# The memory's layer norm in a PSUM bank, in three vector operations instead of two

## The chip, the cores and the metric

The kernel runs on one NeuronCore of a Trainium2 chip. The metric is the device time of one execution, in microseconds (us), lower is better. The engines are PE (TensorE: matmuls and transposes), DVE (VectorE), ACT (ScalarE), POOL (GpSimd) and SP (SyncE, which only issues DMAs). Each engine works through its own instructions in order and waits on semaphores. SBUF is the on-chip memory of 128 partitions; PSUM is a smaller one, in banks of 512 floats for each partition, into which PE writes.

## The reference

Two blocks follow each other: four layers with attention, attention to a fixed memory and a SwiGLU, then two layers of three gated attentions. All is float32, over 256 tokens of width 1024. What the change touches is the very first step on the memory (256 rows of width 1024), whose result all four layers of the first block use for keys and values:

```python
def layer_norm(x, g, b):
    xf = x.astype(jnp.float32)
    mu = jnp.mean(xf, -1, keepdims=True)
    var = jnp.mean(jnp.square(xf - mu), -1, keepdims=True)
    return ((xf - mu) * lax.rsqrt(var + LN_EPS) * g + b).astype(x.dtype)
...
m = layer_norm(mem, mem_ln_g, mem_ln_b)
# in each layer: m @ w_mem_kv[l] gives the keys and values of 4 heads
```

## The kernel before

Rows (tokens or memory rows) lie in two tiles of 128 partitions, `t` 0 and 1. Weights stream from HBM in *units* of two blocks of 128 rows by up to 512 columns. For a unit, SP loads `raw`; ACT rounds it into `w_hi` (task `split`, L1211); POOL takes the difference into `w_lo` (task `low`, two instructions of L1183 for a unit, each with both inputs in SBUF); PE multiplies it (task `products`, for each tile: L1417, L1418 and L1424, six matmuls). Unit n's load waits for the products of unit n-10, its split for those of unit n-8. An activation enters PE through a `turn_in` (four transposes, L1364, into one of two banks `tps`), ACT's `batch_hi` (L1219) and DVE's `take` (L1694).

Units 0 to 3 are the index queries (512 wide), 4 to 7 the index keys (328 wide), 8 to 11 a block of values (512), 12 to 15 the memory's keys and values for the first layer (512), 16 to 23 heads 256 wide.

The order of the work is not written by hand. `Plan.arrange` is a list scheduler: it knows a cost for each task and which tasks it follows, and takes again and again the task that can begin first (then by `prio`, then by its number) and puts it at the end of its engine's queue. A task that has a `room` must also find a bank that is free in the plan. The chip then runs these queues in order. Planned times steer only the order.

The memory's norm, `norm_tiles("mem_norm", ...)`, has for each tile a task `mem_norm_scale` (statistics and a Newton square root in tiny operations, L1813, L1585 to L1587, L1530 to L1534), then for each half of 512 columns a task `mem_norm` of two `scalar_tensor_tensor` (L1594, L1595), in place in the buffer of the memory's rows, which is the trace's `QT`. Each half is followed by a `turn_in`. In the plan before (planned times), DVE has: `mem_norm_scale` of tile 0, the first index queries' take, the index keys' evict and scale of tile 0, then `mem_norm` halves 0 and 1 at 29.91 to 31.51 and to 33.11, the index keys' evict and scale of tile 1, the take of the memory's first turn. PE has after unit 7's products of tile 1 (to 31.83): `turn_in` of the memory's half 0, unit 10 tile 0, unit 8 tile 1, unit 11 tile 0, unit 9 tile 1, `turn_in` of half 1, units 12 and 13 tile 0, unit 10 tile 1, unit 14 tile 0, unit 11 tile 1, `turn_in` of tile 1's half 0, unit 15 tile 0, `turn_in` of its half 1, units 12 and 13 tile 1, unit 16. Further on come eight index groups (L1376), whose scores DVE sums and searches in eight rounds for the top 64 (L1779 to L1802).

Of the kernel before, what the change touches and what calls it, by code (L numbers as in the profile page):

```python
# [11 lines left out]
ALU = mybir.AluOpType  # L12
# [4 lines left out]
T = 2  # L17
# [534 lines left out]
def plan(w):  # L552
# [8 lines left out]
    def norm_tiles(fn, gain, fed, source, chunks=None, keep=False, also=((), ()), scale=2300, apply=1600, acts="x"):  # L561


        done, taken = [], []
        for t in range(T):
            banks = [ch.units[0].mm[t] for ch in chunks] if chunks else None
            st = dict(t=t, gain=gain, banks=banks, keep=keep)
            first = p.task("DVE", "stage", Stage(fn + "_scale", fed[t], **st), scale, None, [*fed[t], *taken], prio=t - 1 if fn == "rms_pre" else 0)
            halves = []
            for half in range(2):  # L570
                one = p.stage(apply, fn, [gain.load, first, *also[t]], prio=t - 1 if fn == "rms_pre" else 0, half=half, **st)
                halves.append(one)
                if chunks and not keep:
                    banks[half].release = one
                if source is not None:
                    clear = [p.used["x"][t]] if acts == "x" else []
                    taken.append(p.tile_batches(source, 4 * half, 4, acts, 4 * half, t, [one], clear)[0].take)
            done.append(halves)
        gain.rest = [halves[1] for halves in done]
        if acts == "x":  # L580
            p.normed = len(p.units)
        return done
# [8 lines left out]
    for t in range(T):  # L591
# [7 lines left out]
    mem = p.task("SP", "mem", None, 3000, "mem_landed", prio=0, lat=2500, inc=16)  # L599
    g = p.gain("mem_ln_g", "mem_ln_b", None)  # L600
    g.load.prio = 0
    constants = p.task("SP", "constants", None, 500 * CONSTANTS, "prologue_landed", [g.load], prio=0, lat=8000,
                       inc=16 * CONSTANTS)
    norm_tiles("mem_norm", g, [[mem]] * T, "mem", scale=2500, acts="m")
    terms = p.task("DVE", "table_terms", None, 1200, "lambda_terms", [constants])
    powers = p.task("ACT", "table_exp", None, 1600, "lambda_exp", [terms])
    lambdas = p.task("DVE", "table_lambda", None, 700, "lambda_done", [powers])
# [8 lines left out]
    for l in range(DEPTH):  # L616
# [21 lines left out]
        if kind == 0:  # L638
# [3 lines left out]
            for t in range(T):  # L642
                bank = last.units[0].mm[t]
                st = dict(t=t, src=src, layer=j, banks=[bank])
                scale = p.task("DVE", "stage", Stage("index_keys_scale", [last.take[t]], **st), 2300, None,
                               [last.take[t]], prio=0)
# [58 lines left out]
        if kind == 1:  # L705
            steps = []
            for b in range(4):
# [4 lines left out]
                                  v=[(src, 2 * MIX + P * whole, P, 0, 0, 0),  # L712
                                     (src, 2 * MIX + P * part + at, HD, 0, 1, at)],
# [41 lines left out]
        g = p.gain("ln1_g", "ln1_b", l, vq[-1].units[-1].load)  # L755
        spec = [(c, n, "residual", c) for c, n in column_chunks(0, D)]
        if kind == 1:
            out = lin(w["w_out"][l], 8, "mixed", spec[:1], banks=[[(3,)], [(0,), (1,), (2,)]], hold=[[p.units[-1].mm[1]], [scored]],
                      rows=MIXED)
        else:  # L760
            out = lin(w["w_out"][l], 8, "mixed", spec[:1], banks=[[(0,)], [(1,)]], rows=MIXED)
        out += lin(w["w_out"][l], 8, "mixed", spec[1:], hold=[[scored]] * T, banks=ANY, rows=MIXED, closing=True)
        norm_tiles("layer_norm", g, [[ch.take[t] for ch in out] for t in range(T)], "x", out)


# [13 lines left out]
        g = p.gain("ln2_g", "ln2_b", l, up.units[-1].load)  # L779
# [5 lines left out]
        if l < DEPTH - 1:  # L785
            norm_tiles("layer_norm", g, fed, "x", down)
        else:
            ready = norm_tiles("layer_norm", g, fed, None, down, keep=True, apply=2300)
            x_in_banks = down
# [4 lines left out]
    for l in range(DEPTH_2):  # L794
        win = w["w_in_2"][l]
        g = p.gain("norm_pre_2", None, l, apart=[memory_last] if l == 0 else ())
# [18 lines left out]
        def branch(weight, mixed, gates, first, fed):  # L815
# [5 lines left out]
            for ci, (c, n) in enumerate(column_chunks(0, D)):  # L821
# [14 lines left out]
                      v=[(da, 1024 + P * i)], out=P * i, dv=P, flavour="differential", mask="bias",  # L836
# [11 lines left out]
        scale = p.task("DVE", "stage", Stage("latent_scale", bq.take, src=low, layer=l), 3400, None, bq.take)  # L848
# [5 lines left out]
        for t in range(T):  # L854
# [14 lines left out]
                      v=[(vm, HD * (2 * i + m), HD, m, 0, HD * m) for m in range(2)], out=[(0, i, 0, P)], scale=MLA_SCALE,  # L869
                      mask="causal", block=2, layer=l, mask_at=bias, z=(low, 416), z_fed=takes(bz))  # L870
                 for i in range(4)]
        for s in steps:
# [16 lines left out]
                      v=[(sw, 640 + HD * (i // 2), HD, m, 0, HD * m) for m in range(2)], out=[(0, i, 0, P)],  # L889
# [16 lines left out]
        g = p.gain("norm_post_2", None, l)  # L906
# [30 lines left out]
def build(nc, a, out):  # L937

    p = plan(a)
    order = p.order  # L940
    rel_rows = nc.dram_tensor("rel_rows", [BIAS_HEADS, P, REL_ROW], F32, kind="Internal").ap()

    with ExitStack() as ctx:
# [78 lines left out]
        ops = ctx.enter_context(nc.psum_tensor("ops", [P, 2, 512], F32))  # L1022
# [13 lines left out]
        def rows(src):  # L1036

            if src == "x":
                return x[:]
            if src == "tmp":  # L1040
                return tmp[:].rearrange("p (t c) -> p t c", t=T)
            if src == "H":
                return H[:]
            if src == "Y":
                return Y[:]
            if src == "mem":
                return QT[:].rearrange("p (t k) n -> p t (k n)", t=T)
            if src == "KI":
                return KI[:].rearrange("p (t c) -> p t c", t=T)
            if src == "MKV":  # L1050
                return MKV[:].rearrange("p (t c) -> p t c", t=T)
            name, cols, off = src
            buf = {"U": U, "tmp": tmp}[name]
            return buf[:, off:off + T * cols].rearrange("p (t c) -> p t c", t=T)
# [463 lines left out]
        def _(dve):  # L1518
            v = nc.vector
            chain = [0]  # L1520

            def link(ins):

                chain[0] += 1
                ins.then_inc(S["dve_chain"], 1)
                dve.wait_ge(S["dve_chain"], chain[0])
# [39 lines left out]
            HALF = (slice(0, D // 2), slice(D // 2, D))  # L1566
# [5 lines left out]
            def halves(g, half):  # L1572
                return [one if one is None else one[:, HALF[half]] for one in gains(g)]

            def norm_columns(t, keys):


                if keys:
                    return small[:, 7, 2 * t:2 * t + 2], small[:, 2, 2 + t:3 + t]
                return mean_var[:, 2 * t:2 * t + 2], rs[:, t:t + 1]  # L1580
# [9 lines left out]
            def norm_apply(t, src, dst, g, done=None, back=None, keys=False):  # L1590

                gg, bb = g
                mv, r = norm_columns(t, keys)
                link(v.scalar_tensor_tensor(out=src, in0=src, scalar=mv[:, 0:1], in1=gg, op0=ALU.subtract, op1=ALU.mult))  # L1594
                ins = v.scalar_tensor_tensor(out=dst, in0=src, scalar=r, in1=bb, op0=ALU.mult, op1=ALU.add)  # L1595
                if back is not None:
                    link(ins)
                    ins = v.bn_stats(back, dst)
                if done is not None:
                    ins.then_inc(done, 1)  # L1600
                else:
                    link(ins)
# [10 lines left out]
            def in_bank(st):  # L1613

                return acc[:, st.banks[-1 if len(st.banks) == 1 else st.half].slot[0], :]
# [69 lines left out]
            def gains(g):  # L1685
                dve.wait_ge(gain_landed[g.slot], g.need)
                return (Y[:, 0, :], None) if g.slot else (gain[:, 0, :], gain[:, 1, :])
# [116 lines left out]
            def do_stage(st, n):  # L1804
                done = S["stage"]
# [3 lines left out]
                fn, t = st.fn, st.t  # L1809
                if fn == "mem_norm_scale":  # L1810
                    m = rows("mem")
# [2 lines left out]
                    link(ins)  # L1814
                    norm_scale(t, stats[:, t, :, :])
                elif fn == "mem_norm":
                    m = rows("mem")[:, t, HALF[st.half]]
                    norm_apply(t, m, m, halves(st.gain, st.half), done)
                elif fn == "layer_norm_scale":
                    norm_scale(t, stats[:, t, :, :])  # L1820
                elif fn == "layer_norm":
# [22 lines left out]
                elif fn == "rms_post":  # L1844
                    z, c = in_bank(st), HALF[st.half]
# [18 lines left out]
                elif fn == "gain_z":  # L1864
                    z = rows(st.src)[:, t, 1536:2048].rearrange("p (h e) -> p h e", e=P)
# [4 lines left out]
                elif fn == "latent_scale":  # L1870
                    mv = small[:, 4, 0:4 * T]
# [217 lines left out]
```

## Time and profile before

| what | us |
|---|---|
| median of 3 runs | 1919.36 |
| lowest and highest | 1918.63, 1919.83 |
| the profiled execution | 1918.94 |
| its span, first to last instruction | 1917.1 |
| PE busy | 1867.1 (97%) |
| POOL busy | 1517.8 (79%) |
| ACT busy | 945.5 (49%) |
| DVE busy | 805.3 (42%) |

The span is what the engines' instructions cover, and the profiled execution has 1.8 us around it. A line such as `L1594 DVE SCALAR_TENSOR_TENSOR QT<-QT,small,gain` names the line of the kernel, the engine, the operation, and the buffer written and those read. `QT`, `L`, `U`, `small`, `gain`, `raw`, `x_rows` lie in SBUF; `acc`, `tps`, `ops` in PSUM.

### The profile page before, as it was taken

Reading aid. Unit: us, or ns where it says so; the run is one execution under the profiler, and the core shown is the slowest. Engines: PE = TensorE matmul, PEld = TensorE weight load, DVE = VectorE, ACT = ScalarE, POOL = GpSimd, SP = SyncE. Lnnn points to the kernel's source line nnn. Section 1 sums busy time; section 2 is a strip of 40 time slices with the busy share of each in tenths; the row PEclk is TensorE's granted clock in tenths of the full one; section 3 lists DMA queues with packets and bytes.
Section 4 is the critical chain, followed back from the end, with each engine's and each line's share of the span. In section 5 each row is a group of like instructions: output and inputs, shape, how many; then the busy total and the mean of one; then the engine's idle time right before and its main releaser. Section 6 shows DMA issues by size and latency. Waiting matters only on the chain.

```text
span 1917.1 us, 27395 instructions
## 1 busy us (share of the span) xinstructions
PE 1867.1 (97%) x9610; PEld 1529.6 (80%) x9610; DVE 805.3 (42%) x1929; ACT 945.5 (49%) x1501; POOL 1517.8 (79%) x1330
## 2 busy tenths in 40 slices
PE   7999999999999999999999999999999999999999
PEld 6778888877888887788888678887787887788877
DVE  6784110446311155411146741106757445455534
ACT  3554444354444355444435644434656654555743
POOL 6768989884897977698987779797686887777785
PEclk9999999999999999999999999999999999999999
DMA  8454656563766554465655456655564564555453
GB/s 274 132 153 149 194 154 232 180 194 102 208 196 214 176 187 139 145 189 147 238 161 149 153 163 186 196 195 166 173 181 130 157 205 153 164 170 176 132 175 110
DMA packets 184557, 330.54 MB, mean 172 GB/s; under 512 B 12220, under 2 KB 44520, under 8 KB 184424
## 3 DMA queue, kind: packets, MB, share of 16 engines
q1 hardware_dynamic: 176512, 323.21, 54.4%
q10 hardware_dynamic: 7912, 5.59, 1.0%
q8 instruction: 80, 1.31, 0.3%
q14 instruction: 53, 0.43, 0.1%
HBM read 325.35 MB, written 3.41 MB: 171 GB/s over the span
## 4 chain that ended last, share of the span: by engine, by line
PE 84%; POOL 5%; DVE 5%; DMA 2%; ACT 2%; issue 2%; SPq 0%; DVEq 0%; ACTq 0%
PE acc L1417 24%; PE acc L1418 23%; PE acc L1424 21%; POOL w_lo L1183 5%; PE tps L1364 4%; PE acc L1439 2%; PE acc L1420 2%; PE ops L1481 2%; PE tps L1457 2%; DMA raw<-in_w_down 1%; PE acc L1388 1%; PE acc L1390 1%; PE acc L1389 1%; DVE QT L1594 1%; PE ops L1376 1%
## 5 line engine op out<-in xcount | busy, mean ns | idle before, releaser
L1183 POOL TENSOR_TENSOR w_lo<-raw,w_hi 128x512 fp32r<-128x512 f32 (+2 forms) x1242 | 1476.8, 1226 | 358.8 <-ACT w_hi L1211 357.4
L1211 ACT CAST w_hi<-raw 128x1024 fp32r<-128x1024 f32 (+3 forms) x624 | 616.3, 991 | 745.7 <-PE acc L1424 560.4
L1417 PE MATMUL acc<-w_hi,xT_hi 128*128 128x512 f32 (+1 forms) x1808 | 687.0, 384 | 4.9 <-ACT U L1245 3.0
L1418 PE MATMUL acc<-w_lo,xT_hi 128*128 128x512 f32 (+1 forms) x1808 | 667.5, 373 | 0.0
L1424 PE MATMUL acc<-w_hi,xT_lo 128*128 128x512 f32 (+2 forms) x1744 | 505.3, 371 | 0.0
L1417 PEld LDWEIGHTS acc<-w_hi,xT_hi 128*128 128x128 f32 x1808 | 341.8, 189 | 74.3 <-issue 14.5
L1418 PEld LDWEIGHTS acc<-w_lo,xT_hi 128*128 128x128 f32 x1808 | 342.4, 189 | 52.6
L1424 PEld LDWEIGHTS acc<-w_hi,xT_lo 128*128 128x128 f32 x1744 | 318.2, 189 | 58.4 <-DVE xT_lo L1694 1.2
L1754 DVE TENSOR_TENSOR H<-G,acc 128x512 f32<-128x512 f32 (+1 forms) x48 | 30.9, 643 | 332.7 <-PE acc L1424 332.7
L1417 PE MATMUL acc<-w_hi,hT_hi 128*128 128x512 f32 x352 | 139.6, 396 | 3.4 <-POOL w_lo L1183 3.4
L1418 PE MATMUL acc<-w_lo,hT_hi 128*128 128x512 f32 x352 | 137.3, 390 | 0.0
L1424 PE MATMUL acc<-w_hi,hT_lo 128*128 128x512 f32 x352 | 108.5, 389 | 0.0
L1747 DVE SCALAR_TENSOR_TENSOR acc<-x_rows,acc 128x512 f32<-128x512 f32 x32 | 22.2, 694 | 201.1 <-PE acc L1424 175.8
L1265 ACT ACTIVATE L<-L,neg_max 128x128 f32<-128x128 f32 (+2 forms) x208 | 96.2, 464 | 11.6 <-DVE neg_max L1935 8.5
L1417 PEld LDWEIGHTS acc<-w_hi,hT_hi 128*128 128x128 f32 x352 | 66.1, 188 | 21.6 <-issue 8.9
L1417 PE MATMUL acc<-w_hi,sT_hi 128*128 128x512 f32 (+1 forms) x200 | 78.9, 395 | 2.9 <-DVE MKV L1744 2.0
L1424 PEld LDWEIGHTS acc<-w_hi,hT_lo 128*128 128x128 f32 x352 | 66.1, 188 | 14.2
L1418 PE MATMUL acc<-w_lo,sT_hi 128*128 128x512 f32 (+1 forms) x200 | 77.3, 387 | 0.0
L1418 PEld LDWEIGHTS acc<-w_lo,hT_hi 128*128 128x128 f32 x352 | 66.1, 188 | 12.7
L1694 DVE TENSOR_TENSOR hT_lo<-tps,hT_hi 128x512 fp32r<-128x512 f32 (+1 forms) x48 | 31.1, 647 | 95.4 <-ACT hT_hi L1219 95.4
L1977 DVE COPY PT<-tps 128x384 f32<-128x384 f32 (+1 forms) x96 | 53.2, 574 | 42.0 <-PE tps L1457 30.9
L1194 POOL TENSOR_TENSOR L<-L,recips 128x128 f32<-128x128 f32 (+1 forms) x84 | 42.4, 529 | 27.5 <-DVE recips L1965 27.4
(209 smaller groups left out, 1998.8 us busy)
## 6 DMA issues: line engine op xcount, KB each, us to landing
raw<-in_w_gate_up SPq DMA_DIRECT2D x160, 512.0 KB, 4.0
raw<-in_w_in SPq DMA_DIRECT2D x104, 512.0 KB, 4.1
raw<-in_w_down SPq DMA_DIRECT2D x88, 512.0 KB, 4.1
raw<-in_w_out SPq DMA_DIRECT2D x48, 512.0 KB, 3.4
raw<-in_w_in_a SPq DMA_DIRECT2D x32, 512.0 KB, 3.9
raw<-in_w_in_b SPq DMA_DIRECT2D x20, 512.0 KB, 4.4
raw<-in_w_mem_kv SPq DMA_DIRECT2D x16, 512.0 KB, 4.1
raw<-in_w_gate_up SPq DMA_DIRECT2D x32, 256.0 KB, 2.8
```

The costliest lines, as they stand in the source:

```text
L1183: ins = nc.gpsimd.tensor_tensor(w_lo[:, r, i, 0:ch.width], raw[:, r, i, 0:ch.width], w_hi[:, slot, i, 0:ch.width].bitcast(F32), ALU.subtract)
L1194: ins = nc.gpsimd.tensor_tensor(part, part, by, ALU.mult)
L1211: nc.scalar.copy(w_hi[:, u.u % SPLIT, 0:u.nk, 0:u.chunk.width], raw[:, u.u % RAW, 0:u.nk, 0:u.chunk.width]).then_inc(S["hi_ready"], 1)
L1265: ins = nc.scalar.activation(part, part, ACT.Exp, bias=neg_max[:, slot, c:c + 1], accum_out=sums[:, slot, c:c + 1])
L1364: ins = nc.tensor.transpose(tps[0:width, k.slot[0], P * i:P * i + P], rows(src)[:, t, col:col + width], ident[:])
L1417: nc.tensor.matmul(o, hi[:, tok], wh, start=first_k, stop=False)
L1418: ins = nc.tensor.matmul(o, hi[:, tok], wl, start=False, stop=False)
L1420: ins = nc.tensor.matmul(o, lo[:, tok], wh, start=False, stop=last_k)
L1424: ins = nc.tensor.matmul(acc[:, bank, 0:ch.width], act_tile(ch.acts, u.k0 + i)[1][:, P * t:P * t + P], w_hi[:, u.u % SPLIT, i, 0:ch.width] ...
L1439: ins = nc.tensor.matmul(acc[:, k.slot[m], c], QT[base:base + n, qt, P * t:P * t + P], KT[kbase:kbase + n, kt, 0:c.stop - c.start], start= ...
L1457: ins = nc.tensor.transpose(tps[:, k.slot[0], P * i:P * i + P], lg[:, j, P * i:P * i + P], ident[:])
L1977: v.tensor_copy(PT[:, j, 0:blocks * P], tps[:, s.turn[j].slot[0], 0:blocks * P]).then_inc(S["t_taken"], 1)
```

## The change

`mem_norm` no longer uses two operations that each read two SBUF tensors (rows and gain, then rows and bias). It uses three, with an intermediate `z` in one bank of `ops`: subtract the mean and multiply by the inverse deviation into the bank, multiply by the gain in the bank, add the bias back into the rows. Each has at most one tensor operand in SBUF. The task's planned cost goes from 1600 to 2300, it claims bank 1 of `ops` in the plan from its begin to its own end, and it waits for the tasks that held the bank.

```diff
@@ norm_tiles
                 halves.append(one)
+                if fn == "mem_norm":
+                    one.room, one.release, one.it.banks = ("ops", [(1,)]), one, [one]
@@ plan
-    norm_tiles("mem_norm", g, [[mem]] * T, "mem", scale=2500, acts="m")
+    norm_tiles("mem_norm", g, [[mem]] * T, "mem", scale=2500, apply=2300, acts="m")
@@ do_stage
                 elif fn == "mem_norm":
-                    m = rows("mem")[:, t, HALF[st.half]]
-                    norm_apply(t, m, m, halves(st.gain, st.half), done)
+                    m, (gg, bb) = rows("mem")[:, t, HALF[st.half]], halves(st.gain, st.half)
+                    mv, r = norm_columns(t, False)
+                    z = ops[:, st.banks[0].slot[0], :]
+                    for h in st.banks[0].held:
+                        dve.wait_ge(S[h.sem], h.n)
+                    link(v.tensor_scalar(z, m, mv[:, 0:1], r, ALU.subtract, ALU.mult))
+                    link(v.tensor_tensor(z, z, gg, ALU.mult))
+                    v.tensor_tensor(m, z, bb, ALU.add).then_inc(done, 1)
```

## Rows read from the trace of the kernel before

**Rows 1.** The page, busy time of an engine, its share and instructions.

```profile
PE 1867.1 (97%) x9610; PEld 1529.6 (80%) x9610; DVE 805.3 (42%) x1929; ACT 945.5 (49%) x1501; POOL 1517.8 (79%) x1330
```

**Rows 2.** Two stretches: us, busy time by engine, granted clock, DMA share, GB/s.

```profile
33.70:42.10 8.40, 0.03 (x1) 0.06 (x1) 8.37 (x3) 0.00 (x0) 6.89 (x6) 0.75 0.88 240
42.10:45.20 3.10, 3.10 (x11) 2.63 (x12) 2.85 (x12) 0.59 (x1) 0.00 (x0) 0.57 0.14 51
```

**Rows 3.** PE's waits over the whole span: us in total, times, longest.

```profile
PE tps L1364 <- DVE QT L1595: 9.3, 3, 8.4
PE tps L1364 <- DVE tmp L1841: 5.0, 2, 2.5
```

**Rows 4.** DVE's timeline, first `mem_norm` half: start us, us, instruction.

```profile
32.38 8.76 DVE L1594 SCALAR_TENSOR_TENSOR QT<-QT,small,gain 128x512 f32<-128x512 f32 x1
41.17 0.75 DVE L1595 SCALAR_TENSOR_TENSOR QT<-QT,small,gain 128x512 f32<-128x512 f32 x1
```

**Rows 5.** POOL's timeline from 8 us on: one unbroken run, and its last instruction.

```profile
11.42 29.17 POOL L1183 TENSOR_TENSOR w_lo<-raw,w_hi 128x512 fp32r<-128x512 f32 x26 [10.98 <-ACT w_hi L1211]
...
39.29 1.30 POOL L1183 TENSOR_TENSOR w_lo<-raw,w_hi 128x512 fp32r<-128x512 f32 x1
```

**Rows 6.** Single lines of DVE: count, duration ns min/median/max, first and last start.

```profile
L1594 DVE SCALAR_TENSOR_TENSOR acc<-acc,small,gain x32: 742/751/759, 166.0 to 1314.9; 128x512 f32<-128x512 f32 x32
L1747 DVE SCALAR_TENSOR_TENSOR acc<-x_rows,acc x32: 685/695/697, 155.3 to 1307.8; 128x512 f32<-128x512 f32 x32
L1646 DVE TENSOR_SCALAR ops<-L x2: 220/224/229, 11.3 to 11.6; 128x8 f32<-128x8 f32 x2
L1802 DVE TENSOR_TENSOR selected<-selected,masks x2: 1533/1534/1534, 118.3 to 1066.8; 128x384 f32<-128x384 f32 x2
L1956 DVE TENSOR_TENSOR L<-L x4: 549/558/1672, 435.9 to 455.4; 128x384 f32<-128x384 f32 x4
```

**Rows 7.** DVE's timeline, later tasks of its queue.

```profile
43.29 0.16 DVE L1740 TENSOR_SCALAR U<-acc 128x8 f32<-128x8 f32 x1
...
43.95 0.18 DVE L1585 BATCH_NORM_AGGREGATE small<-small 128x2 f32<-128x6 f32 x1
...
46.28 0.69 DVE L1694 TENSOR_TENSOR mT_lo<-tps,mT_hi 128x512 fp32r<-128x512 f32 x1
...
51.16 1.27 DVE L1813 BATCH_NORM_STATS2 stats<-QT 128x6 f32<-128x512 f32 x2
...
54.83 1.21 DVE L1594 SCALAR_TENSOR_TENSOR QT<-QT,small,gain 128x512 f32<-128x512 f32 x1
...
59.40 0.70 DVE L1664 TENSOR_SCALAR neg_sinks<-sinks 128x16 f32<-128x16 f32 x1
...
60.79 0.68 DVE L1694 TENSOR_TENSOR mT_lo<-tps,mT_hi 128x512 fp32r<-128x512 f32 x1
61.39 0.28 DVE L1594 SCALAR_TENSOR_TENSOR acc<-acc,small,knorm 128x64 f32<-128x64 f32 x1
```

**Rows 8.** The chain that ended last, from the memory's first turn on.

```profile
42.07 1.09 PE tps L1364 x4
...
44.87 0.49 PE acc L1424 x2
46.28 0.45 PE acc L1424 x2
```

**Rows 9.** DMA issues: KB each, us to landing; first the gain's, then unit 14's.

```profile
gain<-in_mem_ln_g SPq DMA_DIRECT2D x1, 512.0 KB, 11.3
...
raw<-in_w_mem_kv SPq DMA_DIRECT2D x1, 512.0 KB, 12.9
```
**Rows 10.** SP's queue: start us, us, issue.

```profile
11.83 0.75 SPq L1134 DMA_DIRECT2D gain<-in_mem_ln_g  x1
...
28.84 4.24 SPq L1146 DMA_DIRECT2D raw<-in_w_mem_kv  x2
```

**Rows 11.** ACT's timeline, one split of a unit.

```profile
48.62 1.04 ACT L1211 CAST w_hi<-raw 128x1024 fp32r<-128x1024 f32 x1
```

## The prediction

> **What bounds the kernel now.** I read the page first: PE is busy for 1867.1 of 1917.1 us [rows 1], so only work that leaves PE idle, or slow, can be worth anything. Then PE's waits, longest in total first: one line stands out, `turn_in` of the memory (L1364) waiting for the norm (L1595), 9.3 us in three waits, 8.4 of them in one; no other line has more than 5.0 us, nor a single wait over 2.5 [rows 3] (leaving out the start, before anything has landed). The table by stretches puts the long wait between 33.7 and 42.1 us: PE does 0.03 us of work there, DVE is "busy" all through it, and the granted clock falls to 0.75; in the 3.1 us behind it, it is 0.57, which is mostly the lower of TensorE's two levels (1.2 instead of 2.4 GHz), after 8.4 us in which PE did nothing [rows 2].
>
> DVE's timeline shows why. The first of the norm's operations lasts 8.76 us, from 32.38 to 41.14; the three that follow, of the same form, last 0.75 (the first of them stands for all three) [rows 4]. POOL runs without a gap from 11.42 to 40.59 (11.42 + 29.17) [rows 5], and the operation ends 0.55 us after POOL's last instruction. Was it waiting for data? The gain was issued at 11.83 and landed 11.3 us later, long before [rows 9, 10]. So I read it as two engines wanting one way into SBUF: an operation with two SBUF tensors cannot stream while POOL's instructions, also with two, follow each other back to back.
>
> **Is that so for operands in a bank?** 32 operations of the same line with one input in a bank and one in SBUF lie between 742 and 759 ns, 32 of L1747 between 685 and 697 [rows 6], although POOL is busy 79% of the span [rows 1]. None was ever held. Those with two SBUF inputs vary: L1956 from 549 to 1672 ns, L1802 1533 for only 384 columns [rows 6]. Nothing else comes near 8.76, though; a wait of one POOL instruction (1.2 us or so) is the rule, and why this one lasted through seven is not in the trace.
>
> The Trainium skill (SBUF — State Buffer, Who interferes with whom) says that VectorE and GpSimd share a port pair as an exclusive lock held for one instruction, and that a VectorE instruction with at most one SBUF input outside the two-port modes does not contend. The second half agrees with the tight 742 to 759 [rows 6]. The first, taken alone, would hold the norm for one POOL instruction, not seven: by it the same kernel would have little to gain, but the 8.76 us row contradicts it, and the row decides.
>
> **The change, part by part.** *Operations.* Removed: 4 at tile 0 (8.76 + 3 x 0.75) and 4 at tile 1, which run from 54.83 to 59.40, 4.57 us, beside POOL [rows 7]. Added: 12 operations of 512 columns, one operand in a bank. The two multiplications and additions cost what L1747 does, 0.69. The first form, SBUF to a bank with column scalars, does not occur at this width; its nearest row is L1646, 8 columns, 0.22 us at most 0.23 with POOL already running [rows 6]. Bounds: 0.69 if it streams like the others, and, were it held like the two-operand form, the whole of the wait. I take 0.69. With 0.03 us between linked operations (41.14 to 41.17 [rows 4]) a half is 3 x 0.72 = 2.15 us, a tile 4.3.
>
> *The waits for the bank* are on a half that DVE itself finished just before; bank 1 has no earlier holder in the plan. Behind them on DVE nothing else is delayed. 0 to 0.1 us each, hidden in the 2.15.
>
> *The order.* The higher cost moves things in the plan; I walked it. Half 0 ends at 32.21 in plan instead of 31.51, after PE is free at 31.83, so unit 10's tile 0 goes ahead of the memory's first turn: useful, since on the chip its `w_lo` is there at 33.2 (POOL's twentieth instruction; six remain at about 1.23 us before 40.59 [rows 5]) and it covers 1.37 us. The takes of the memory's turns go ahead of the index keys' evict and scale of tile 1, the second turn ahead of unit 9's tile 1, and a take of index queries falls behind tile 1's norm. It is needed only by the index groups. Nothing is moved on SP or POOL up to there.
>
> *The chain on DVE.* 32.38; tile 0's two halves to 36.7; take 0.65 to 37.35; evict of index keys 0.66 (43.29 to 43.95) to 38.0; their scale 2.33 (43.95 to 46.28) to 40.35; take 0.65 to 41.0; tile 1's scale 3.67 (51.16 to 54.83) to 44.65; its halves 4.3 to 48.95; two takes 1.3 to 50.25; the table terms 1.39 (59.40 to 60.79) to 51.65. There the next task (index keys, L1594) starts, which before starts at 61.39 [rows 7]: 9.7 us earlier.
>
> *The chain on PE.* Idle removed: 8.4. Slow clock removed: the turn and unit 10's products take 42.07 to 45.36 (44.87 + 0.49), 3.29 us; the next products take 45.36 to 46.73, 1.37, and a turn at full clock 0.45 [rows 8], so 1.82 would do: 1.5 saved. Waits for tile 1's halves (9.3 - 8.4 [rows 3]): 0.9, gone, since DVE is through at 46.8 and 48.95 and PE comes at about 48 and 51. Sum 10.8. What is late next: unit 14's weights. Issued at 28.84, landed 12.9 later, at 41.7 [rows 9, 10], whatever PE does. Split 1.04 to 42.8 [rows 11], POOL 2.5 to 45.3; PE, at 1.37 a product from 33.7 with two turns between, wants it at 44.1. A new wait of 1.2. Net 9.6. Both chains agree.
>
> *The rest of the run.* From 63.5 on the same work with the same buffers follows, all of it paced by PE's own progress, so the lead is kept as far as the order is kept. The order beyond 47 us of the plan will differ somewhere; I can't bound that from rows except by the largest single wait, 2.5 us either way [rows 3].
>
> The profiled execution is 1918.94, 0.4 under the median of 1919.36. 1919.4 - 9.6 = 1909.8.
>
> **Rivals.**
> 1. *Less comes through (0.13).* The freed order collides with the DMA queue or POOL: units 15 and on are issued after unit 14 and land after it [rows 10]; if each of two or three made PE wait as unit 14 does, or if one task in the new order cost the largest wait seen, the gain is 9.6 - 2.5 to 9.6 - 5: 1912.3 to 1914.8. For it: DMA is at 0.88 until 42 us [rows 2]. Against: POOL alone needs 2.5 us for a unit against 2.7 on PE.
> 2. *The operation is held all the same (0.05).* If a bank as output does not free the first operation, it ends at 41.14 as now, the half 1.45 later at 42.6 instead of 41.9: 0.7 lost, tile 1 gives back 0.3. 1919 to 1920.5. For it: 8.76 us is unlike every other row, so its cause may be another. Against: its end with POOL's end, and 64 tight rows.
> 3. *Slower (0.04).* The reshuffled order puts a task that DVE's search for the top 64 needs behind others; its end gates the masks of six attention steps. To be slower by over 0.2% it must eat 9.6 and 3.8 more, 13.4 us, five times the largest later wait: 1923 or more. Nothing in the trace speaks for it but that the planner may do as it likes.
> 4. *More (0.03).* Tile 1's norm no longer slows POOL's lows (54.83 to 59.40), and with it a wait or two of PE later on: 1907 or below.
>
> **How the numbers follow.** The forecast has 0.75, 1907 to 1912.3 by the 2.5 us either side. The range for 8 in 10 reaches into rival 1 and a bit into 4: 1906 to 1913.8. What this kernel's measurement can tell from no change is about 0.2%, 3.8 us: faster covers the forecast, rivals 1 and 4 (0.91, less a little of rival 1's unlucky end: 0.90), same rival 2 (0.06), slower rival 3 (0.04).
>
> **What would show it.** In the profile after, the three operations should last 0.65 to 0.75 each, beside a POOL that runs on to about 40.6; PE should have no gap over 1.5 us between 33.7 and 63, the clock 1.00 throughout, and the first turn of `QT` at about 35. Index keys' L1594 should start near 51.7. The prediction is wrong if the first operation is long again, if PE's wait turns up at unit 14 or 15 with more than 2 us, or if PE's idle time after 63 us grows by more than 3.

## The result, and the profile after

The changed kernel takes 1909.09 us (median of 6 runs, 1907.14 to 1910.85), the one before 1919.59 over the 6 runs now made of it (1917.43 to 1921.59). The ratio is 0.9945, with a 95% interval of 0.9933 to 0.9958: 10.5 us less, where 9.6 was forecast, and the time lies 0.7 us under the predicted 1909.8. The profiled execution is 1908.38 with a span of 1906.5; before it was 1918.94 with 1917.1.

DVE's timeline of the kernel after, where tile 0 is normed (start us, us, instruction), to be held against [rows 4]:

```profile
32.08 0.81 DVE L1824 TENSOR_SCALAR ops<-QT,small 128x512 f32<-128x512 f32 x1
32.93 0.70 DVE L1825 TENSOR_TENSOR ops<-ops,gain 128x512 f32<-128x512 f32 x1
33.66 0.69 DVE L1826 TENSOR_TENSOR QT<-ops,gain 128x512 f32<-128x512 f32 x1
...
52.94 0.29 DVE L1596 SCALAR_TENSOR_TENSOR acc<-acc,small,knorm 128x64 f32<-128x64 f32 x1
```

The 8.76 us operation is gone; three take its place and end 2.3 us after the first began. POOL runs beside them exactly as it did, for 29.34 us without a gap; then it pauses, 2.27 us instead of 9.15:

```profile
11.29 29.34 POOL L1185 TENSOR_TENSOR w_lo<-raw,w_hi 128x512 fp32r<-128x512 f32 x26 [10.85 <-ACT w_hi L1213]
42.89 12.18 POOL L1185 TENSOR_TENSOR w_lo<-raw,w_hi 128x512 fp32r<-128x512 f32 x14 [2.27 <-ACT w_hi L1213]
```

PE's waits in the first 62 us, after; and the stretches, to be held against [rows 2]:

```profile
PE tps L1366 <- DMA ident<-in_c_ident: 4.7, 1, 4.7
PE acc L1419 <- POOL w_lo L1185: 1.6, 1, 1.6
PE tps L1366 <- DMA x_rows<-in_x: 1.1, 1, 1.1
```

```profile
35.20:42.10 6.90, 6.90 (x35) 5.71 (x34) 6.45 (x19) 2.00 (x4) 5.42 (x5) 1.00 0.95 284
42.10:53.50 11.40, 9.83 (x54) 8.11 (x53) 10.30 (x23) 6.61 (x11) 10.61 (x12) 1.00 0.35 97
```

The 9.3 us of waits for the norm have left the list [rows 3]. Between 35.2 and 42.1 PE is busy all the time and the granted clock is 1.00; before, it was 0.75 between 33.7 and 42.1 and then 0.57. One new wait has come, 1.6 us, and the chain that ended last, from 28.57 on, names all its links:

```profile
28.57 13.17 DMA raw<-in_w_mem_kv
41.74 0.02 issue
41.77 1.06 ACT w_hi L1213
42.83 0.07 issue
42.89 2.54 POOL w_lo L1185 x2
45.43 0.14 issue
45.57 0.47 PE acc L1419
```

That is unit 14: its weights land at 41.74, whatever PE does before. It is what sets the time now at this place.

PE's turns and unit 10's products, in the new order (timeline of after):

```profile
33.28 0.47 PE L1419 MATMUL acc<-w_hi,xT_hi 128*128 128x512 f32 x1
...
34.74 0.60 PE L1366 MATMUL tps<-ident,QT 128*128 128x128 f32 x4
...
37.93 0.60 PE L1366 MATMUL tps<-ident,QT 128*128 128x128 f32 x4
```

How far the lead is kept can be read from one line that runs all through the first block, with its first and last start; first before, then after:

```profile
L1595 DVE SCALAR_TENSOR_TENSOR x_rows<-acc,small,gain x28: 750/751/753, 166.8 to 1123.2; 128x512 f32<-128x512 f32 x28
```

```profile
L1597 DVE SCALAR_TENSOR_TENSOR x_rows<-acc,small,gain x28: 750/751/752, 157.7 to 1112.3; 128x512 f32<-128x512 f32 x28
```

9.1 us at 160 us, 10.9 at 1120. The queues of PE differ last at their entry 69 of 1657, which is planned at 72.7 us and runs at 85.8 in the kernel before and at 77.4 in the changed one; behind it the order is the same in both. The 1.8 us between the two readings is no effect of the change that I can name; single runs of either kernel lie up to 4 us apart.

### The profile page after: what moved, and what is told of

Its sections match the earlier page's. It is cut to its first block, busy times and chain, and to the rows that moved or that the text cites. A ratio compares the mean times of both kernels' runs of the same rounds, so it can differ in the third digit from the quotient of the medians.

```text
span 1906.5 us, 27403 instructions
## 1 busy us (share of the span) xinstructions
PE 1865.8 (98%) x9610; PEld 1529.7 (80%) x9610; DVE 798.1 (42%) x1933; ACT 945.2 (50%) x1501; POOL 1516.2 (80%) x1330
## 4 chain that ended last, share of the span: by engine, by line
PE 84%; POOL 6%; DVE 4%; DMA 3%; ACT 2%; issue 1%; SPq 0%; DVEq 0%; ACTq 0%
PE acc L1419 24%; PE acc L1420 23%; PE acc L1426 21%; POOL w_lo L1185 6%; PE tps L1366 4%; PE acc L1441 2%; PE acc L1422 2%; PE ops L1483 2%; PE tps L1459 2%; DMA raw<-in_w_down 1%; PE acc L1390 1%; PE acc L1392 1%; PE acc L1391 1%; DMA raw<-in_w_mem_kv 1%; PE ops L1378 1%
```

## The experiments

Twelve kernels. "Held" means that the first operation on the memory's rows lasts as long as POOL's run. Each time is compared with runs of the kernel before on the same chip, whose medians were 1919.5 to 1920.8. Seven of the twelve (e3, e4, e5, e6, e9, e11, e12) have a single execution, so their times have no interval; what they show rests on durations in their traces, of 1 to 10 us.

### Operations and order, one at a time

**e1_order_only**: the planned cost, the claimed bank and the waits stay; the operations are the old ones.

```diff
-                    link(v.tensor_scalar(z, m, mv[:, 0:1], r, ALU.subtract, ALU.mult))
-                    link(v.tensor_tensor(z, z, gg, ALU.mult))
-                    v.tensor_tensor(m, z, bb, ALU.add).then_inc(done, 1)
+                    norm_apply(t, m, m, (gg, bb), done)
```

> The changed kernel's planned order, claimed bank and waits, but the two old operations in place, with two SBUF tensors each. Theory (the operands decide): the first operation is held until POOL's run ends near 40.6, about 8.8 us long, as before; only unit 10's products (1.4 us) now cover part of the wait, so PE idles about 7 us at the memory's first turn: 1917 to 1918.5. Rival (the new order is what gains): about 1909, with no long operation.

1918.13 us, ratio 0.9993 (0.9983 to 1.0002). The new order alone gives nothing that can be told from zero. The operation is held, for 9.16 us, and PE waits for it:

```profile
31.83 9.16 DVE L1596 SCALAR_TENSOR_TENSOR QT<-QT,small,gain 128x512 f32<-128x512 f32 x1
```

```profile
PE tps L1366 <- DVE QT L1597: 7.1, 1, 7.1
```

**e10_ops_old_order**: the kernel before with the three operations written into bank 1 directly, so that all queues keep their old order, entry for entry.

```diff
-                    m = rows("mem")[:, t, HALF[st.half]]
-                    norm_apply(t, m, m, halves(st.gain, st.half), done)
+                    m, (gg, bb) = rows("mem")[:, t, HALF[st.half]], halves(st.gain, st.half)
+                    mv, r = norm_columns(t, False)
+                    z = ops[:, 1, :]
+                    if n > 1:
+                        dve.wait_ge(done, n - 1)
+                    link(v.tensor_scalar(z, m, mv[:, 0:1], r, ALU.subtract, ALU.mult))
+                    link(v.tensor_tensor(z, z, gg, ALU.mult))
+                    v.tensor_tensor(m, z, bb, ALU.add).then_inc(done, 1)
```

> The kernel before with the three operations in bank 1 and the queues exactly in the old order (no cost changed, no bank claimed in the plan). Theory (the operations carry nearly all, the order only covers PE's wait of about 0.7 us for the first half and some at tile 1): PE idles 0.7 to 1 us at the first turn, 1910 to 1912. Rival (as the kernel with the cost at 1600 came out at 1916, the gain needs the new order): 1914 or more.

1912.47 us, ratio 0.9957 (0.9944 to 0.9971), some 8 us of the 10.5. PE's waits for the norm are small but there, which the order of the changed kernel covers with unit 10's products:

```profile
PE tps L1364 <- DVE QT L1824: 2.8, 3, 1.5
```

It is 0.5 above the range of 1910 to 1912. Its interval overlaps that of the changed kernel, so that the order adds 2 us is what the medians and these waits say, not what the intervals prove.

**e2_cost_1600**: the changed kernel with `apply=1600`.

> The changed kernel with the task's planned cost back at 1600, so the queue's order is about that of before, with the three operations in the bank. Theory: nearly all of the gain stays; PE reaches the memory's first turn at 33.4 and waits some 1 us for the first half at 34.3: 1909 to 1911. Rival (the order carries the gain): 1915 or more.

1916.01 us (1912.23 to 1916.72), ratio 0.9977 (0.9966 to 0.9988): outside what the theory gave, on the rival's side. The operations are as fast as in the changed kernel (0.81, 0.70, 0.69, none held). My premise was wrong: the order is not that of before. The claimed bank alone moves things: PE's queue has another task than before at 89 of its entries, the last of them entry 141, where the changed kernel's has at 28, the last of them entry 69. PE's idle time in the profile is 1912.8 - 1867.7 = 45.1 us against 1906.5 - 1865.8 = 40.7. There is no one wait; the lead over before is 8.3 us when the top 64 are found (110.0 against 118.3 [rows 6]) and 4.9 at the first norm after:

```profile
L1597 DVE SCALAR_TENSOR_TENSOR x_rows<-acc,small,gain x28: 749/751/752, 161.9 to 1118.0; 128x512 f32<-128x512 f32 x28
```

So with the same operations this order costs 4 us against the old one (e10) and 6 to 7 against that of the changed kernel, by ratios and medians; the one with the truer cost (2300 for 2.3 us) is the better one here. Which of the moved tasks costs it is not shown.

**e7_tile0_only**: three operations at tile 0, the two old ones at tile 1 (`if t == 0: ... else: norm_apply(t, m, m, (gg, bb), done)`).

> The changed kernel with the three operations at tile 0 only; tile 1 has the two old ones. Theory (all the gain is in tile 0's first operation): 1908.5 to 1910.5, with tile 1's four operations 0.75 to 1.25 us each. Rival (a large wait appears at tile 1 as well now that POOL runs 512 wide low parts there, 42.9 to 48): one operation of several us, 1912 or more.

1910.97 us, ratio 0.9948 (0.9934 to 0.9961), not to be told from the changed kernel. The gain is in tile 0. Tile 1's old operations last 1.67, 1.67, 1.18 and 1.12, two of them over the 1.25 that the theory allowed: beside an unbroken POOL run, and 512 wide instructions at first, and yet each is let in after one of POOL's.

```profile
44.25 1.67 DVE L1596 SCALAR_TENSOR_TENSOR QT<-QT,small,gain 128x512 f32<-128x512 f32 x1
45.96 1.67 DVE L1597 SCALAR_TENSOR_TENSOR QT<-QT,small,gain 128x512 f32<-128x512 f32 x1
```

### Which operation is held

**e3_two_inputs_to_bank**: two operations, the first with rows and gain from SBUF into the bank.

```diff
+                    link(v.scalar_tensor_tensor(out=z, in0=m, scalar=mv[:, 0:1], in1=gg, op0=ALU.subtract, op1=ALU.mult))
+                    v.scalar_tensor_tensor(out=m, in0=z, scalar=r, in1=bb, op0=ALU.mult, op1=ALU.add).then_inc(done, 1)
```

> The changed kernel with two operations: the first reads rows and gain, both in SBUF, and writes the bank; the second reads the bank and the bias and writes SBUF. Theory (two SBUF inputs are what is held): the first operation still lasts to the end of POOL's run, 8 us or more, the second is 0.75: about 1917. Rival (only an SBUF output in the same operation is held): no long operation, two operations of 0.75, and a time of 1909 or a little under.

1917.97 us, held:

```profile
32.69 9.16 DVE L1824 SCALAR_TENSOR_TENSOR ops<-QT,small,gain 128x512 f32<-128x512 f32 x1
41.89 0.75 DVE L1825 SCALAR_TENSOR_TENSOR QT<-ops,small,gain 128x512 f32<-128x512 f32 x1
```

A bank as output does not help; two SBUF inputs are enough to be held.

**e4_scale_in_sbuf**: the scaling stays in SBUF, then a copy into the bank, then the two others.

```diff
-                    link(v.tensor_scalar(z, m, mv[:, 0:1], r, ALU.subtract, ALU.mult))
+                    link(v.tensor_scalar(m, m, mv[:, 0:1], r, ALU.subtract, ALU.mult))
+                    link(v.tensor_copy(z, m))
```

> The changed kernel with the first operation (one SBUF tensor, column scalars) writing back into SBUF instead of the bank, then a copy of it to the bank, then the two others: four operations. Theory by which any operation that uses the second way into SBUF is held (the Trainium skill, SBUF — State Buffer, counts a column-scalar operation from SBUF to SBUF among them): it is held like the old one until about 40.6: 1917 to 1918. Rival (only two tensor inputs are held): it lasts 0.3 to 0.8 us, four operations 2.6 us a half: about 1910.

1918.96 us, 1 above the theory's range, held, although the operation has a single tensor operand in SBUF; its fellow at half 1, after POOL's run, is the fastest of all:

```profile
32.34 8.81 DVE L1824 TENSOR_SCALAR QT<-QT,small 128x512 f32<-128x512 f32 x1
41.18 0.69 DVE L1825 COPY ops<-QT 128x512 f32<-128x512 f32 x1
...
43.78 0.53 DVE L1824 TENSOR_SCALAR QT<-QT,small 128x512 f32<-128x512 f32 x1
```

By this and e3, what frees the first operation of the change is both: one tensor in, and that into a bank. The Trainium skill (SBUF — State Buffer, Who interferes with whom) lists as contending with GpSimd an instruction with two SBUF inputs, where GpSimd's reads SBUF, and column-scalar operations when they can use two ports; these runs agree (9.16 us in e3 and 8.81 in e4, against 0.81 in the changed kernel).

### Why it was held through seven instructions

**e5_pool_pauses**: the kernel before; POOL waits for tile 0's second half before unit 11's low part.

```diff
+            normed = [k.n for k in order["DVE"] if k.kind == "stage" and k.it.fn == "mem_norm"]
...
+                if u.u == 11:
+                    pool.wait_ge(S["stage"], normed[1])
                 pool.wait_ge(S["hi_ready"], u.split.n)
```

> The kernel before, with one wait added: POOL does not begin unit 11's low part before tile 0's second norm half is done. Theory (POOL's unbroken run holds the operation): the first operation ends about 0.6 us after POOL stops near 33.2, so lasts about 1.4 us instead of 8.8; the others 0.75; POOL resumes near 36; PE idles about 1 us at the turn and about 1 at unit 11: 1910 to 1912. Rival (something else, such as the constants' DMAs landing until about 40, holds it): still 8 us or more, and as POOL would then wait too, 1925 or more.

1912.77 us, 0.8 above the theory's range. The first operation lasts 1.11 us instead of 8.76:

```profile
32.67 1.11 DVE L1598 SCALAR_TENSOR_TENSOR QT<-QT,small,gain 128x512 f32<-128x512 f32 x1
33.81 0.75 DVE L1599 SCALAR_TENSOR_TENSOR QT<-QT,small,gain 128x512 f32<-128x512 f32 x1
```

POOL's unbroken run is the cause: nothing but POOL's wait was added.

**e6_pool_256**: the low parts of units 10 to 13 in instructions of 256 columns.

```diff
+                step = 256 if 10 <= u.u <= 13 else ch.width
                 for i in range(u.nk):
-                    ins = nc.gpsimd.tensor_tensor(w_lo[:, r, i, 0:ch.width], raw[:, r, i, 0:ch.width],
-                                                  w_hi[:, slot, i, 0:ch.width].bitcast(F32), ALU.subtract)
+                    for c in range(0, ch.width, step):
+                        ins = nc.gpsimd.tensor_tensor(w_lo[:, r, i, c:c + step], raw[:, r, i, c:c + step],
+                                                      w_hi[:, slot, i, c:c + step].bitcast(F32), ALU.subtract)
```

> The kernel before, with the low parts of units 10 to 13 in instructions of 256 columns instead of 512, back to back as before. Theory 1 (the wait grew to seven instructions because long ones leave no opening; beside 256 wide ones the same operations take 1.2 us at tile 1): the first operation lasts 1 to 2 us, time 1910 to 1912. Theory 2 (any unbroken run of POOL can hold it, by chance of the phase): it lasts to the end of POOL's run, now near 41.5, and the time is 1919 to 1921.

1921.88 us, 0.9 above the second theory's range; held for 10.25 us, to the end of a POOL run that is longer by 1. The length of POOL's instructions isn't it.

```profile
32.14 10.25 DVE L1596 SCALAR_TENSOR_TENSOR QT<-QT,small,gain 128x512 f32<-128x512 f32 x1
```

**e11_held_later_phase**: one operation of 0.7 us on DVE ahead of the first held one (`link(v.bn_stats(stats[:, t, 0, :], m))`, its result unused).

> The kernel before with one statistics operation of 0.7 us (one SBUF tensor, result not used) put in front of the first held operation, so that it asks half a POOL instruction later. Theory (an unbroken run holds it whenever it asks): first operation 8.0 to 8.2 us long, still ending near POOL's end, time as before, 1918 to 1921. Rival (the phase in which it asks decides, and elsewhere it gets in after one instruction): 1.2 to 2 us, time 1911 to 1913.

1917.44 us; the operation asks at 33.05 instead of 32.38 and is held for 8.40 us, to 41.45. POOL's run began 0.28 later here (11.70), so against POOL's own instructions the request moved by 0.36 us, not by half of one. The other traces fill this in: operations that were held asked 0.53 to 1.25 us before the end of the 512 wide POOL instruction then running (before, e1, e3, e4, e9, e11), and those that were let in at its end, at tile 1, asked 0.45 to 1.13 us before it (e1, e3, e5, e7). The moment at which it asks isn't it either.

**e9_held_constants_later**: e1 with the constants' DMAs behind the weights of units 14 and on (`prio=2`).

> The order-only kernel (old operations, new order) with the constants' load issued behind the weights of units 14 and on, which lets POOL run unbroken beyond 40.6 (with the three operations it ran to about 50). Theory (the operation is held as long as POOL's run has no break): it is held beyond 41, to the end of the longer run, 14 to 18 us long, and the time is 1923 to 1928. Rival (the constants' DMAs, landing from 24 to 40 us, have a part in the hold, or it is let in after some bound of its own): it ends by 42, time 1918 or less.

1919.3 us, held for 8.90 us. POOL's run was no longer than in e1 (29.22 us, ending at 40.93), because ACT, which must split unit 14 first, stands in its own queue behind the memory's turn; so the longer hold that the theory forecast could not occur, and that half of the expectation stays untried. The rival's half on the constants is answered: from 32.5 to 40.5 us the DMA engines are busy for 0.25 of the time instead of 0.95 in e1, and the hold is the same. A bound of its own on the hold is not excluded.

**e12_pool_waits_for_itself**: the kernel before; POOL waits for its own completed low part ahead of units 11 to 13.

```diff
+                if 11 <= u.u <= 13:
+                    pool.wait_ge(S["lo_ready"], p.units[u.u - 1].low.n)
                 pool.wait_ge(S["hi_ready"], u.split.n)
```

> The kernel before with POOL made to wait, ahead of the low parts of units 11, 12 and 13, for its own low part of the unit in front to be complete; nothing else is changed, and POOL loses perhaps 0.1 us at each. Theory (the hold needs POOL's instructions issued with no opening between them): the first operation is let in at the first such wait, near 33.2, and lasts about 1.4 us; 1910 to 1913. Rival (a gap that small is not enough): 8.8 to 9.2 us, 1919 to 1921.

1914.11 us, 1 above the theory's range. The first operation is let in at the first such wait; DVE and POOL then take turns, and POOL's instructions start 1.4 to 1.8 us apart instead of 1.24:

```profile
32.38 1.81 DVE L1596 SCALAR_TENSOR_TENSOR QT<-QT,small,gain 128x512 f32<-128x512 f32 x1
34.23 1.63 DVE L1597 SCALAR_TENSOR_TENSOR QT<-QT,small,gain 128x512 f32<-128x512 f32 x1
35.78 1.77 DVE L1596 SCALAR_TENSOR_TENSOR QT<-QT,small,gain 128x512 f32<-128x512 f32 x1
37.59 1.65 DVE L1597 SCALAR_TENSOR_TENSOR QT<-QT,small,gain 128x512 f32<-128x512 f32 x1
```

So the long hold needs POOL's instructions to come one behind the other with no wait that takes effect between them. That is necessary, not sufficient. In this same run the second and the fourth operation got in between the two instructions of one unit, where POOL has no wait. And at tile 1 the old operations got in after one instruction beside an unbroken POOL, in e7 and within kernels that held the first one at tile 0; this is e1, 9.16 us at tile 0:

```profile
53.52 1.67 DVE L1597 SCALAR_TENSOR_TENSOR QT<-QT,small,gain 128x512 f32<-128x512 f32 x1
```

What makes the difference between the two stays open.

### What is late next

**e8_constants_later**: the changed kernel with the constants' load at `prio=2`.

> The changed kernel with the load of the eight constants given a later priority, so that it is issued behind the weights of units 14 and on. Theory (what is late next is unit 14's weights, landing at 41.8, and PE's wait of 1.6 us for them): unit 14 lands by about 38, POOL runs on without its pause of 2.3 us, the wait goes: 1907 to 1908. Rival (the constants are then late for the index keys or the table terms at about 51, or nothing changes because the queue's bandwidth is the limit): 1909 or more.

1909.41 us, ratio 0.994 (0.9926 to 0.9953): no different from the changed kernel. The mechanism worked, POOL ran on to 50.15 and of the 1.6 us at unit 14 nothing is left but 0.4:

```profile
PE acc L1419 <- POOL w_lo L1185: 0.4, 1, 0.4
```

```profile
11.61 38.54 POOL L1185 TENSOR_TENSOR w_lo<-raw,w_hi 128x512 fp32r<-128x512 f32 x36 [11.17 <-ACT w_hi L1213]
```

But the lead was given back: the end of the lambda table (L1684), 2.1 us earlier than in the changed kernel (55.2 against 57.3), is followed by a search that starts 0.3 earlier (74.7 against 75.0), and the first norm of `x_rows` too (157.4 against 157.7). 0.3 us can't be measured in this kernel. The forecast of 1907 to 1908 fell.

## Why the prediction was right, point by point

- **The bound.** It lay in PE's one long wait; the waits for the norm, 9.3 us, have gone, and 1.6 at unit 14 has come: 7.7 less. PE's idle time fell by more, 9.3 (1917.1 - 1867.1 = 50.0 before, 1906.5 - 1865.8 = 40.7 after); that it is again 9.3 is chance. The other 1.6 us are spread over small waits, 1.0 of them behind 160 us, and no run ties them to the change. With 1.3 less busy time that is 10.6, the difference of the spans; the named terms alone make 9.0.
- **The cause of the 8.76 us.** Read from its end with POOL's end and from the 64 tight rows; shown by e5 and e12 (a pause of POOL, and a wait of POOL for itself, end it) and by e3 and e4 (both kinds of operands that are held). That one POOL instruction would be the rule, and seven the exception, holds too: tile 1 in e7. Why seven stays open, as the prediction had it.
- **The three operations.** 0.69 each was right for two. The first form, from SBUF into a bank with column scalars, was mis-sized, 0.81: a half is 2.27 us, not 2.15. "Each 0.65 to 0.75" failed there.
- **The order.** As walked: unit 10's tile 0 ahead of the first turn, the first turn at 34.74 ("about 35"), the second ahead of unit 9's tile 1. I gave it cover of a short wait and no more, and e1 and e10 agree. What I did not see is how much another order can cost (e2), though rival 1 allowed for it.
- **The slow clock.** 1.5 us forecast, 1.3 less busy time seen, and the clock is 1.00 from 33.7 to 53.5. The 0.45 us for a turn at full clock does not stand in [rows 8], whose 0.45 is that of two matmuls; the trace after bears it out: the first turn and the products behind it take 34.74 to 36.57, 1.83 us, where 1.82 was forecast.
- **Late next.** Unit 14's weights, named beforehand: a wait of 1.2 forecast, 1.57 measured, from a landing at 41.74 (41.7 forecast) to PE's start at 45.57. It is just over the 1.5 us that the prediction gave as the largest gap.
- **DVE's chain.** Index keys forecast to begin at 51.65 ("near 51.7"), begun at 52.94. At tile 1's norm DVE was still 0.45 us ahead (44.20 against 44.65), in spite of the longer first operations. Then a take waited 0.46 for ACT, an evict of the memory's values was put ahead (0.6), and the table terms took 1.9 instead of 1.39, as one with two SBUF inputs lasted 1.03 (L1669) where it had lasted 0.41. The takes and tile 1's norm add about 0.2. PE did not wait for any of it, having other products first, so this miss cost nothing; that both chains agreed at 9.6 was partly luck.
- **The rest.** 9.1 us of lead at 160 us where 9.6 was forecast, close to the 9.0 of the named terms; 10.5 at the end by the medians. What lies between is not explained.

Of the rivals, the second (held all the same) fell with the first row after; the third had nothing for it. Of the fourth, the first half was seen: in e7 the old operations at tile 1 stretch two of POOL's instructions from 1.27 to 1.74 us. But e7's time can't be told from that of the changed kernel, so it was worth nothing that these runs can measure.

## What to carry to other kernels

Look at each vector operation's single durations, not at a group's mean: some 8 of the 10 us sat in one instruction of 1929. Where POOL has a stretch of instructions that wait for nothing, let no operation on the critical chain read two SBUF tensors, or go from SBUF to SBUF with column scalars; through a PSUM bank, three operations of 0.7 to 0.8 us were held in none of these runs, at the price of one more operation. This rests on one stretch of one kernel; elsewhere the same operations lost only one of POOL's instructions. And before such an edit, read the queues for what is late next (here DMAs issued long before) and give the list scheduler true costs, since its order can take back more than half of a gain.

## What the runs showed of the hardware

- A VectorE operation was held not for one GpSimd instruction but for seven or more in a row: 8.40 to 10.25 us in seven kernels (before, e1, e3, e4, e6, e9 and e11), always to 0.3 (e4) or 0.55 us (the others) after the end of GpSimd's last. Narrower GpSimd instructions and a request 0.7 us later changed nothing; a wait of GpSimd for its own completed instruction ended it at 1.81 us.
- The same operation beside an unbroken GpSimd run was also let in after one instruction, in a kernel that had held it before (9.16 us at tile 0 and 1.67 at tile 1 in e1; 8.76 and 1.21 in the kernel before). Once GpSimd had waited for itself, VectorE got in also between two instructions that had no wait between them (1.63 and 1.65 us, e12). Not explained.
- The column-scalar operation of 512 columns takes 0.53 us from SBUF to SBUF when it is free, and 0.81 from SBUF into a bank.
- GpSimd, whose instructions of 512 columns started 1.22 to 1.25 us apart during the hold and 1.24 to 1.26 before it, was not slowed at all while it held VectorE; taking turns, its starts were 1.4 to 1.8 us apart (e12).
